# Seven block products for a third group of weight rows, with a sixth slot for split weights

## The reference, cut to what matters

```python
def swiglu(h, w_gate_up, w_down):
    gu = h @ w_gate_up                      # 256x2048 @ 2048x11264
    gate, up = gu[..., :D_FF], gu[..., D_FF:]
    return (jax.nn.silu(gate) * up) @ w_down   # D_FF = 5632
...
        x = x + swiglu(rms_norm(x, norm_ffn[l]), w_gate_up[l], w_down[l])
    return rms_norm(x, norm_final)
```

## Time and profile before

| | us |
|---|---|
| median of 3 runs | 1746.3 (1745.05 to 1746.69) |
| the profiled execution | 1746.86 |
| its span, first to last instruction | 1745.1 |
| PE busy | 1729.5 (99%) |
| DVE busy | 1178.7 (68%) |
| ACT busy | 923.3 (53%) |

### The profile page before, as it was taken

How to read it: one execution, slowest core, us unless ns; L and a number is a source line. 1 busy time by engine, 2 the same in 40 slices (tenths; PEclk the granted TensorE clock), 3 DMA queues, 4 the chain that set the end, 5 groups by cost and what they waited for, 6 DMA issues and landing times.

```text
span 1745.1 us, 22788 instructions
## 1 busy us (share of the span) xinstructions
PE 1729.5 (99%) x8701; PEld 1452.2 (83%) x8701; DVE 1178.7 (68%) x1456; ACT 923.3 (53%) x1288; POOL 166.4 (10%) x183
## 2 busy tenths in 40 slices
PE   9999999999999999999999999999999999999998
PEld 8998778888788787888888887888888888888886
DVE  6545765455656677455555558888878788888887
ACT  6334566544553545444444545556566565656654
POOL 1004363000000024000000000001001001001100
PEclk9999999999999999999999999999999999999999
DMA  8754443465586545565556555668669759758752
GB/s 307 244 172 132 146 139 127 132 205 186 155 270 190 165 145 169 158 193 187 189 189 193 179 184 190 220 193 265 232 181 283 242 186 281 235 188 264 238 211 106
DMA packets 198701, 343.40 MB, mean 197 GB/s; under 512 B 6752, under 2 KB 59616, under 8 KB 198112
## 3 DMA queue, kind: packets, MB, share of 16 engines
q1 hardware_dynamic: 186032, 319.49, 54.6%
q0 software_dynamic: 9792, 18.88, 6.1%
q10 hardware_dynamic: 2800, 3.96, 0.7%
HBM read 321.34 MB, written 2.10 MB: 185 GB/s over the span
## 4 chain that ended last, share of the span: by engine, by line
PE 88%; DVE 5%; ACT 2%; issue 2%; DMA 1%; POOL 1%; SPq 1%; POOLq 0%; DVEq 0%; ACTq 0%
PE acc L615 11%; PE acc L617 11%; PE acc L616 11%; PE acc L1068 5%; PE acc L1066 5%; PE acc L657 5%; PE acc L1067 5%; PE acc L1080 4%; PE acc L1082 4%; PE acc L1081 4%; PE acc L658 3%; PE acc L645 2%; PE acc L646 2%; PE acc L644 2%; PE aux L1066 2%
## 5 line engine op out<-in xcount | busy, mean ns | idle before, releaser
L1758 DVE TENSOR_TENSOR wlo<-raw,whi 128x1024 fp32r<-128x1024 f32 x341 | 423.1, 1242 | 359.8 <-ACT whi L1330 356.9
L1330 ACT ACTIVATE whi<-raw 128x1024 fp32r<-128x1024 f32 x341 | 360.6, 1059 | 330.8 <-PE acc L617 222.6
L1675 ACT ACTIVATE whi<-raw 128x1024 fp32r<-128x1024 f32 x300 | 316.7, 1060 | 237.1 <-PE acc L1068 79.2
L2238 DVE TENSOR_TENSOR wlo<-raw,whi 128x1024 fp32r<-128x1024 f32 x300 | 363.8, 1222 | 114.9 <-ACT whi L1675 110.7
L615 PE MATMUL acc<-whi,hboth 128*128 128x512 f32 x432 | 170.8, 395 | 0.0
L617 PE MATMUL acc<-whi,hboth 128*128 128x512 f32 x432 | 168.4, 390 | 0.0
L616 PE MATMUL acc<-wlo,hboth 128*128 128x512 f32 x432 | 168.3, 390 | 0.0
L657 PE MATMUL acc<-hboth,whi 128*128 128x512 f32 x384 | 135.8, 398 | 0.0
L1080 PE MATMUL acc<-whi,fhi 128*128 128x512 f32 x320 | 124.6, 389 | 0.0
L1082 PE MATMUL acc<-whi,flo 128*128 128x512 f32 x320 | 124.5, 389 | 0.0
L1081 PE MATMUL acc<-wlo,fhi 128*128 128x512 f32 x320 | 124.5, 389 | 0.0
(11 more groups left out here) (381 smaller groups left out, 3520.9 us busy)
## 6 DMA issues: line engine op xcount, KB each, us to landing
raw<-w_in SPq DMA_DIRECT2D x112, 1024.0 KB, 5.2
raw<-w_gate_up SPq DMA_DIRECT2D x88, 1024.0 KB, 7.4
raw<-w_down SPq DMA_DIRECT2D x44, 1024.0 KB, 7.3
raw<-w_out SPq DMA_DIRECT2D x32, 1024.0 KB, 5.1
xres<-down POOLq DMA_DIRECT2D x36, 512.0 KB, 9.2
raw<-w_branch_a SPq DMA_DIRECT2D x8, 1024.0 KB, 5.1
raw<-w_branch_b SPq DMA_DIRECT2D x8, 1024.0 KB, 5.2
raw<-w_in SPq DMA_DIRECT2D x5, 512.0 KB, 8.3
```

Source lines behind the costliest of these rows:

```text
L1330: nc.scalar.activation(whi[:, j % 4], raw[:, j // 2, 2 * (j % 2):2 * (j % 2) + 2, :], ACT.Copy).then_inc(hi_ready, 1)
L1675: nc.scalar.activation(ring(x)[0], raw_piece(u, half), ACT.Copy).then_inc(hi_ready, 1)
L1758: nc.vector.tensor_tensor(wlo[:, j % 4], raw[:, j // 2, 2 * (j % 2):2 * (j % 2) + 2, :], whi[:, j % 4].bitcast(F32), ALU.subtract).then_in ...
L2238: nc.vector.tensor_tensor(lo, raw_piece(UNIT[what, r], half), hi.bitcast(F32), ALU.subtract).then_inc(lo_ready, 1)
```

## The change

A third group of four k-tiles goes by seven block products. `ORDER` now holds 4 plain pieces and 21 of the groups (`GU` = 25), then 8 down pieces: `NB` = 33. The ring has six slots; since 33 is odd, the loop runs over pairs of bodies with the slots shifted. The last sum v4 is made by DVE for the third group only. For groups 0 and 1 POOL makes it with an adding DMA, raw tile onto raw tile, 4 KB per partition, and ACT waits for its landing (`v4_landed`). `LOADS` maps units to buffers anew, a unit of `up` is free only after v4's piece, and the left sums, formerly two groups wide, are three.

```diff
-ORDER = (("a", 0), ("b", 0), ("g", 0), ("c", 0), ("v1", 0), ("g", 1), ("v2", 0), ("v3", 0), ("u", 0), ("v4", 0), ("u", 1),
...
+ORDER = (("a", 0), ("b", 0), ("g", 0), ("c", 0), ("v1", 0), ("g", 1), ("v2", 0), ("u", 0), ("v3", 0),
+         ("a", 1), ("b", 1), ("v4", 0), ("c", 1), ("u", 1), ("v1", 1), ("v2", 1), ("v3", 1),
+         ("a", 2), ("v4", 1), ("b", 2), ("c", 2), ("v1", 2), ("v2", 2), ("v3", 2), ("v4", 2))
 ORDER += tuple(("d", n) for n in range(8))
-GU = 22
+GU = 25
 NB = len(ORDER)
-SLOTS = 5
+GROUPS = 3
+SLOTS = 6
...
+LOADS = (("gate", 1, 4), ("up", 1, 5), ("gate", 0, 0), ("up", 0, 1), ("gate", 2, 2), ("up", 2, 3), ("gate", 3, 0), ("up", 3, 5),
+         ("down", 0, 4), ("down", 1, 1), ("down", 2, 2), ("down", 3, 3))
...
+    if what == "up" and r in (1, 2):
+        return AT["v4", r - 1]
     return max(x for x, op in enumerate(ORDER) if home_of(op)[:2] == (what, r))
...
-        shi = place("shi", [P, 4, 4, P], F32R, at=o_r)
-        slo = place("slo", [P, 4, 4, P], F32R, at=o_r + 8192)
+        shi = place("shi", [P, 4, 2 * GROUPS, P], F32R, at=o_r)
+        slo = place("slo", [P, 4, 2 * GROUPS, P], F32R, at=o_r + 12288)
...
+            body(0, 0)
+            with pe.Fori(0, FF_BODIES // 2 - 1) as r:
+                body(2 * r + 1, 1)
+                body(2 * r + 2, 0)
+            body(FF_BODIES - 1, 1)
...
+                if op in (("v4", 0), ("v4", 1)):
+                    act.wait_ge(v4_landed, 32 * i + 16 * op[1] + 16)
...
-                    act.wait_ge(piece_used, B0 + NB * i + x - 4)
-                nc.scalar.activation(ring(x)[0], raw_piece(u, half), ACT.Copy).then_inc(hi_ready, 1)
+                    act.wait_ge(piece_used, B0 + NB * i + x - 5)
+                nc.scalar.activation(ring(x, odd)[0], raw_piece(u, half), ACT.Copy).then_inc(hi_ready, 1)
...
-                    if x == 27:
+                    if x == 31:
                         act.wait_ge(combined, 7 * i + 6)
...
-                    if x == 28 and not last:
+                    if x == 32 and not last:
                         down_copy(i, 0)
...
-                    if x == 19:
+                    if x == 24:
                         combine(1, i)
-                    if x == 23:
+                    if x == 26:
                         combine(2, i)
-                    if x == 24:
+                    if x == 28:
                         combine(3, i)
                         combine(4, i)
-                    if x == 25:
+                    if x == 29:
                         combine(5, i)
-                    if x == 26:
+                    if x == 30:
                         combine(6, i)
                         combine(7, i)
-                    if x == 28:
+                    if x == 31:
                         product(i)
...
+                    if last and x == 32:
...
+                        down_add(0)
...
+            def last_sum(i, n):
+
+                pool.wait_ge(sums_made, 10 * i + 3 * n + 3)
+                pool.dma_start(raw_piece(UNIT["gate", 1 + n], 1), raw_piece(UNIT["up", 1 + n], 1), accum_op=ALU.add).then_inc(v4_landed, 16)
...
+            for i in range(FF_BODIES):
+                if i:
+                    down_sum(i - 1, 1)
+                    down_sum(i - 1, 2)
+                last_sum(i, 0)
+                if i:
+                    down_sum(i - 1, 3)
+                last_sum(i, 1)
+                if i < FF_BODIES - 1:
+                    down_sum(i, 0)
```

More of the change, by code:

```diff
@@ L1057, in d_stat, with into @@
             def d_stat(kt, i):
-                return dhi[:, kt, :], dlo[:, kt, :]
-            def into(x, bank, stat, kt0, i, last=True):
+                return hhi[:, HOLES[kt], P:TOK], hlo[:, HOLES[kt], P:TOK]
+            def into(x, odd, bank, stat, kt0, i, last=True):
                 q = [name for name in qbank if qbank[name] is bank]
-                hi, lo = ring(x)
+                hi, lo = ring(x, odd)
                 for k in range(2):
@@ L1103, in body @@
                         if first:
-                            pe.wait_ge(s_ready, 2)
+                            pe.wait_ge(s_ready, 1)
                         else:
                             pe.wait_ge(down_copied, 4 * i)
+                    if first and x == AT["u", 0]:
+                        pe.wait_ge(s_ready, 2)
                     if x == AT["v3", 0]:
@@ L1652, in _, with hi_part @@
                         act.wait_ge(s_raw, 1)
-                        nc.scalar.activation(dhi[:], draw[:], ACT.Copy).then_inc(s_hi, 1)
+                        for k in range(2):
+                            done = nc.scalar.activation(shi[:, 2 * k:2 * k + 2], sraw[:, 2 * k:2 * k + 2], ACT.Copy)
+                        done.then_inc(s_hi, 1)
             act.wait_ge(s_raw, 2)
-            for k in range(2):
-                done = nc.scalar.activation(shi[:, 2 * k:2 * k + 2], sraw[:, 2 * k:2 * k + 2], ACT.Copy)
-            done.then_inc(s_hi, 1)
-            def hi_part(i, x):
+            act.wait_ge(piece_used, 8 * (Q_FF + 1) + 5)
+            nc.scalar.activation(holes(hhi), draw[:].rearrange("p (a k) c -> p a k c", k=2), ACT.Copy).then_inc(s_hi, 1)
+            def hi_part(i, odd, x):
                 op = ORDER[x]
@@ L2240, in right_sum @@
             def right_sum(kind, n, i):
-                b11, b21 = (raw_piece(UNIT["gate", 2 + n], half) for half in range(2))
-                b12, b22 = (raw_piece(UNIT["up", 2 + n], half) for half in range(2))
-                made = 8 * i + 4 * n
+                b11, b21 = (raw_piece(UNIT["gate", 1 + n], half) for half in range(2))
+                b12, b22 = (raw_piece(UNIT["up", 1 + n], half) for half in range(2))
+                made = 10 * i + 3 * n
                 if kind == "v1":
-                    u = UNIT["up", 2 + n]
-                    dve.wait_ge(raw_in[u], 16 * ((Q_BODY if u < 4 else 0) + 1 + loads_before("up", 2 + n)) + 32 * i)
+                    u = UNIT["up", 1 + n]
+                    dve.wait_ge(raw_in[u], 16 * ((Q_BODY if u < 4 else 0) + 1 + loads_before("up", 1 + n)) + 32 * i)
                     nc.vector.tensor_tensor(b11, b11, b12, ALU.add).then_inc(sums_made, 1)
```

166 lines of the change are left out of this document (80 added, 86 removed).

## The result

The changed kernel takes 1756.8 us (median of 4 runs, 1755.82 to 1758.11) where the kernel before takes 1746.02 (4 runs, 1745.05 to 1746.69). The ratio is 1.0063, with a 95% interval of 1.0045 to 1.008: **slower by 10.8 us**. The prediction was 1741.6 with a range of 1734 to 1755 and an even chance of faster. It was wrong in sign, and the time lies outside the range. The profiled execution took 1756.85 us, its span 1755.1, 10.0 more than in the earlier trace rows.

A forecast was written before the change was run, and what follows sets the result against it. PE was taken to bound the kernel, alone setting a body's length. Profiled 1746.9 - 13.6 + 5.4 + 0.5 + 1 + 2 = 1742.2, less 0.6 to the median of the runs: 1741.6 us, range 1734 to 1755.

The forecast's parts named there:

- What bounds the kernel and what can be won: Feed-forward bodies: PE alone sets the length; 6 fewer matmuls each, floor 62.11 us, ten bodies -13.6 us at most.
- DVE's layout: DVE's order within a body: 55.7 of 62.1 us busy, ahead of PE's needs by 1.6 us at its tightest.
- The new wait, L - 8.2: Group 1's v4 waits for its adding DMA; a body loses L - 8.2 us, L from POOL's start to landing.
- the 17.1: Time from PE's start of piece 0 to POOL's start of group 1's adding DMA, laid out as 17.1 us.
- rival 2: ACT's wait for the landing takes the whole gain and more: 1751 at L = 9.7, 1756 at 10.2; chance 0.26.
- One sign: Expected in the trace: ACT waits 1 to 2.5 us in each body for group 1's adding DMA, none for group 0.
- The value of L: Landing time of group 1's adding DMA, taken as 8.8 us, ends 5.6 and 10.2; nine bodies +5.4 us.
- the first body's +1: First body starts with a smaller lead, DVE reaching c1 some 1.6 us later against PE: +1 us.
- The edges: Outside the regular bodies: +0.5 us ahead of the first body, +1 in the first, +2 in the last.
- the first term: Ahead of the first body: left sums of three groups take DVE 8.0 us for 7.1; +0.5 us.
- The last body: DVE adds part 0 one rest later, behind piece 32, at 52.2 or 54 against d4's 51.2: +2 us.
- Rival 1: Group 1's v4 lands in time, L 5.6 to 8.2, no body waits: -11, 1735 us; chance 0.22 for L below 8.2.

The follow-up runs named there:

- the one with three edits: Changed kernel, group 1's v4 behind c2, part 0's copy ahead of d7's weight copy, last body's DVE add of part 0 one piece earlier: 1733.09 us.

## Why the prediction was wrong, point by point

**What bounds the kernel and what can be won: right.** Six matmuls a body are gone, the pitch is unchanged, and every kernel in which the landing was hidden shows 62.11 us a regular body, the floor to the hundredth.

**DVE's layout: right in what it said of the floor.** It said that the floor can be reached with little room. Five kernels reach it, one of them with another wide instruction. It had one time too early, as the next point shows.

**The new wait, L - 8.2: right in place and slope, its constant 0.45 too high.** The path laid out (landing, ACT, 16 wide and five narrow instructions, silu, copies, d4) is in the trace, and so is the bound at pieces 22 to 25 that stood 0.5 us behind it: in the body shown piece 22 costs more than d4. The eight regular bodies lose 63.84 - 62.11 = 1.73 us with a mean L of 9.48, where L - 8.2 gives 1.28. In the body shown above piece 0 starts on PE at 1339.39. By the layout POOL would start at 1339.39 + 17.1 = 1356.49 and d4 at 1339.39 + 43.0 + 9.27 = 1391.66; the trace has 1356.72 and 1391.90, 0.23 and 0.24 late. The path behind POOL's start is thus as laid out, and the 17.1 in front of it was not.

It is not lead that the body had lost to the landing: in the kernel with v4 two pieces later, at the floor, POOL starts as late. Piece 0 and that DMA in it:

```profile
1328.77 0.39 PE L1076 MATMUL acc<-whi,hboth 128*128 128x512 f32 x1
```

```profile
1346.12 0.90 POOL L2524 DMA_DIRECT2D raw<-raw  x1 [13.69 <-DVE raw L2268]
```

That is 17.35 us. The eight regular bodies have 17.32 to 17.81 there, 17.40 on average, and 17.32 to 17.82 in the changed kernel, 17.43. The layout let DVE take c1's rest as soon as ACT's copy was made, 1.29 us behind PE's start of piece 7. But DVE has a row without a gap there, with two of the second group's sums in it, and c1's rest is the second of these two, at 1354.07; ACT's copy for it began at 1352.73:

```profile
1352.93 2.35 DVE L2253 TENSOR_TENSOR wlo<-raw,whi 128x1024 fp32r<-128x1024 f32 x2
```

```profile
1352.73 1.06 ACT L1691 ACTIVATE whi<-raw 128x1024 fp32r<-128x1024 f32 x1 [0.30 <-PE scores L1078]
```

So 0.33 of the 0.45 is POOL's start, and the other 0.1 is PE's slow second start after the wait at d4. The measured rule is L - 7.75, for an L of 8.6 as of 9.5. No regular body had an L between 6.6 and 7.9, so where the loss begins was not seen. The loop that stood under rival 2 is near the one that the traces show (part 1's landing and part 3's copy, not part 0's and part 2's); it closes at the same length and adds nothing to this path.

One sign was set wrong whatever L is. ACT was to wait 1 to 2.5 us for the landing and waited 4.8. It has nothing left to do 5.2 us behind POOL's start (9.27 + 0.09 - 4.14), so even an L of 8.8 would have given 3.7. The sum does not use it.

**The value of L: the step that failed.** I took 8.8, between 8.4 and 9.7, because the transfer "meets loads for half" of its length. It took 9.1 to 10.6 with a median of 9.6, as long as one that has loads all along. With it the term for the nine bodies, +5.4, was mis-sized: the nine distances exceed the floor by 8 x 1.73 + 3.94 = 17.8 us, where my terms for them (+5.4 and the first body's +1) give 6.4. The number of bytes was the wrong thing to count. Without down 0 and down 1 the same transfer lands in 5.1 us, with down 0 in 8.65: one megabyte issued 1.9 us ahead of POOL costs 3.6 us, and the next, 1.2 us behind it, 0.9 more. The upper end I gave, 10.2, was below what the first two bodies had (10.5 and 10.6). Why those two are longer stays open.

**The edges.** In the kernels with a hidden landing the first d0 is at 1119.3 to 1120.7, against 1121.58 - 1.36 + 0.5 = 1120.7 by the prediction, and the first distance is 62.1 to 63.2 for my 63.1: the first term held to within 0.7 us in four of the five, and the "+1" is there in three of the five (62.7 to 63.2) and gone in the one with the down loads behind the landing and the one with three edits. In the changed kernel they are buried under the long landings of the first two bodies. The last body was named and placed rightly (DVE's add of part 0 in front of d4) and priced at 2 us; with the rest of the body it came to 2.6. PE's timeline, kernel after:

```profile
1714.09 0.50 PE L1090 MATMUL acc<-whi,fhi 128*128 128x512 f32 x1 [2.86 <-DVE xres L2193]
```

**The sum again**, against the 14.7 us by which the profiled execution missed (1756.9 for 1742.2): the eight regular bodies 63.84 for 62.71, of which 0.68 is L and 0.45 the constant, 9.0; up to the first d0 2.7 and the first distance 2.3, both with L at 10.5; the end 0.6. That is 14.6.

**The rivals.** Rival 2 came true by its first mechanism, the landing, and had a chance of 0.26. Its figures were too low as well: L = 9.7 was to give 1751 (that figure counts nine bodies at 1.5 us, though its text says ten), and with 9.6 it is 1756.8, which the rival has for 10.2. The constant and the first two bodies make the difference. Rival 1 is what the experiments with a hidden landing show: 1735 was its figure, 1734.4 to 1735.3 were measured. On the rules of the Trainium skill: "DMA: Bandwidth & Descriptors", section "Anatomy of one DMA — SWDGE (gpsimd) path", would put this transfer at an estimated 3.2 us. The runs do not agree: it took 4.6 us at the least and 9.5 beside loads. "GPSIMD Engine Reference", section 1, "Specifications", speaks of contention on the interfaces that GpSimd shares with VectorE. No run here shows a price: POOL's record of the issue is 0.90 us in the midst of DVE's two-input instructions.

## What to carry to other kernels

A transfer put in the place of an instruction has the latency of the moment at which it is issued, and the loads queued just around it decide that: look at what the load queue issues in the few us before, and take the median of transfers with the same company, not a value between. Where it must be waited for in order, ask how many instructions stand between issue and wait, since each of them pays for its own length; two more pieces between issue and wait were worth 22 us here. And before you remove a wait, look for a second loop through the same landing: here one without PE was as long as the one through it, and removing PE's wait alone won nothing in a regular body.

## What was not expected of the hardware

- The same adding DMA of 512 KB took 4.6 to 5.2 us with one load issued 2.4 us ahead, about 8.65 with two and 9.5 with three. A quarter of its bytes beside three loads took 6.0 to 6.6 us in the regular bodies.
- The three loads issued about POOL's start fared by their order: in the body shown, up 3, issued at 1354.3, landed in 5.0 us, down 0 (1354.9) and down 1 (1357.9) in 9.9 and 10.1. The rows are those of the DMA view, 1354 to 1366 us of the kernel after (KB each, median us to landing):

```profile
raw<-w_down SPq DMA_DIRECT2D x2, 1024.0 KB, 10.0
raw<-w_gate_up SPq DMA_DIRECT2D x1, 1024.0 KB, 5.0
```

- After PE has waited, the distance of the next two starts is 0.33 us where 0.23 is usual, so each wait costs 0.1 us more than its length.
- POOL's record of an adding DMA is 0.90 us for the second group's, with runs of 4 KB, and 1.19 to 1.21 for the down parts with runs of 2 KB. The first group's, issued right behind another, has 1.42.
